# Two blocks of a hybrid network on one core: the order of rounding, scaling and turning the first operand and the state-space output

## The chip, the cores and the metric

The kernel runs on one core of one Trainium2 chip. A time is device microseconds (us) of one execution; three executions give the median. Engines: TensorE (PE, with PEld its weight loads), VectorE (DVE), ScalarE (ACT), GpSimd (POOL) and SyncE (SP), which here issues the loads of the weights.

## The reference

Batch 1, 256 tokens, width 2048, all in float32. Two blocks follow each other. What the change touches lies in the first part of the first block:

```python
a_in = _rmsnorm(h, attn_norm_g)
proj = a_in @ w_in                       # 2048 x (2048 + 3072 + 32 + 3072)
z, xbc, dt_raw, q, k, v = split(proj)
xs, bm, cm = split(silu(causal_dwconv(xbc)))
y = _ssd(xs, dt, a_neg, bm, cm) + d_skip * xs       # 4 groups of 512 channels
y = y * silu(z)
y_ssm = _rmsnorm(y per group of 512, ssm_norm_g)    # one root per token and group
y_att = sliding_window_attention(rmsnorm+rope(q), rmsnorm+rope(k), v)
h = h + concatenate([y_ssm, y_att]) @ w_out
```

After it come a convolved feed-forward layer, a gated embedding, and the second block (gated delta rule, Fourier mixing, MLP). They are not touched.

## The kernel before

**Products.** Every large matrix product is made of float32 values split in two: a rounded part (`hi`, type fp32r) and the rest (`lo`). The weights stream in as 952 slabs of 256 rows by 512 columns (512 KB). A quad is four slabs; `w_raw`, `w_hi` and `w_lo` hold one quad each, so a slab's place is free again when the slab four before it is done. SP loads a slab into `w_raw` once `w_lo` of the slab four before is written. ACT copies `w_raw` to `w_hi` with rounding (`split` on ACT, line 754), DVE subtracts to get `w_lo` (`split` on DVE, line 1341). PE does 12 matmuls of 128x512 per slab (`slab`, lines 2137 and 2142): `hi*hi` and `lo*hi` with `w_hi`, four each, then four with `w_lo`. A chunk is eight slabs: 512 output columns over 2048 rows. The signals `hi_ready`, `lo_ready` and `slab_done` count the slabs, so the order of the calls on ACT and DVE decides in which order slabs and operand tiles come.

**The operand.** The left side of a chunk is `a_hi`, `a_lo`: 16 k-tiles of 128 rows by 256 tokens. `operand_tiles(n, src, ready, i)` on PE turns k-tiles 2i and 2i+1 with four 128x128 transposes (line 2165) into a bank of the accumulator memory; ACT rounds that bank into `a_hi` (`gained`, with the norm's gain, or `rounded_operand`), DVE writes the rest into `a_lo` (`gained_rest` or `rest_of_operand`). The pair of tiles i is the left side of slab i of a chunk. From pair 4 on, PE waits until `a_lo` of pair i-4 is done, since they share a bank. New tiles overwrite the old operand in place.

**The first chunk** (`first_chunk`): PE turns pairs 0 and 1, then for slab s it turns pair s+1 (s from 1 to 6), waits for `a_lo` of pair s, and does slab s. ACT's order is in lines 844 to 851, DVE's in 1459 to 1466. Behind it ACT squares h for the norm, DVE takes the mean, and the narrow product for `dt` (`narrow`) follows.

**The state-space part** runs beside the six chunks of q, k and v (`Q_QKV`), one group g beside chunk g+1. PE calls within a chunk: `decay_rows`, `state` before slab 1, `within(0)` before slab 3, `of_state`, `within(1)` before slab 6. POOL makes `xd`, `xds`, waits for `y_squared`, makes `dx`, multiplies the weights `seg_w` that `within` waits for, and normalizes and rotates q and k (`qk_root`, `qk_scaled`, `qk_rotated`). DVE makes `gated_output(t)` and ACT its square (`square(t)`, sum in `ssm_ss`). When all four groups are squared, POOL takes one root for all (line 637), DVE scales z by root and gain (line 1611), and PE turns z beside the last chunk of v, slabs 3 to 7 (`tiles_of_y`, line 2339). The last pair is turned at the start of the next product, `w_out` (`beside`).

Of the kernel before, what the change touches and what calls it, by code (L numbers as in the profile page):

```python
# [25 lines left out]
ALU = mybir.AluOpType  # L26
# [166 lines left out]
def program(nc, wstream, small, const, out):  # L193

    ctx = ExitStack()
    with ctx:
# [339 lines left out]
        def _(pool):  # L536
# [66 lines left out]
            for g in range(GROUPS):  # L603
# [22 lines left out]
                for t in range(TT):  # L626
# [3 lines left out]
                    if t == 0:  # L630
# [6 lines left out]
            inverse_root(ssm_rs[:].rearrange("p t g -> p (t g)"), ssm_ss[:].rearrange("p t g -> p (t g)"),  # L637
                         TT * GROUPS, 1.0 / NC, EPS, ssm_rstd)
# [108 lines left out]
        def _(act):  # L747
# [217 lines left out]
            split(q + 1, 0, 3)  # L965
            rounded_operand(TR_YSSM, 0, 2)
            split(q + 1, 3, 4)
            rounded_operand(TR_YSSM, 2, 3)
            split(q + 2, 0, 1)
            rounded_operand(TR_YSSM, 3, 5)  # L970
            split(q + 2, 1, 2)
            rounded_operand(TR_YSSM, 5, 6)
            split(q + 2, 2, 3)
            rounded_operand(TR_YSSM, 6, 7)
# [358 lines left out]
        def _(dve):  # L1333
# [125 lines left out]
            gained_rest(TR_ATTN, C_ATTN, 0)  # L1459
            for i in range(QUAD):  # L1460
                gained_rest(TR_ATTN, C_ATTN, i + 1)
                split(0, i, i + 1)
            for i in range(QUAD - 1):
                gained_rest(TR_ATTN, C_ATTN, QUAD + i + 1)
                split(Q_XBC + 1, i, i + 1)
            split(Q_XBC + 1, QUAD - 1, QUAD)
# [100 lines left out]

            def qk_sums(c, t):
# [5 lines left out]
            for g in range(GROUPS):  # L1574
# [24 lines left out]
                gated_output(1)  # L1599
                split(q + 2, 2, 4)  # L1600
# [5 lines left out]
            dve.wait_ge(ssm_rstd, 1)  # L1606
            dve.wait_ge(gain_loaded, 16 * (G_SSM + 1))
            for g in range(GROUPS):
                cols = slice(g * NC, (g + 1) * NC)
                for t in range(TT):  # L1610
                    V.scalar_tensor_tensor(z[:, t, cols], z[:, t, cols], ssm_rs[:, t, g:g + 1], gain[:, cols],
# [1257 lines left out]
```

## Time and profile before

| | before |
|---|---|
| median of 3 runs | 3007.11 us (3005.98 to 3009.41) |
| the profiled execution | 3011.07 us |
| its span | 3009.0 us |
| mean granted TensorE clock | 0.994 |
| PE busy | 2955.5 us (98%) |
| DVE, ACT, POOL busy | 2010.2, 1411.7, 322.5 us |

The profiled execution's own time is its span and some 2 us around it. PE is busy nearly all the time; in the 40 slices of the page only the first is below nine tenths (six), and POOL is busy at eight tenths or more in slices 5 to 7, some 300 to 520 us, where the state-space part runs. PE's busy time does not tell at which clock a matmul ran: the row of the granted clock has 8 tenths in the first slice and 9 in nearly all others.

### The profile page before, as it was taken

The page shows a single profiled execution, that of the slowest core. Times are in us where ns is not written, and L with a number is a line of the kernel's source. Part 1 is how long each engine was busy: PE and PEld are TensorE (multiplying, and loading weights), DVE is VectorE, ACT ScalarE, POOL GpSimd, SP SyncE. Part 2 cuts the span into 40 slices and gives each one's busy share as a digit, 9 for nine tenths or more (in the row PEclk, how much of TensorE's full clock was granted, in tenths as well). Part 3 has the DMA queues.
Part 4 walks back from the last instruction along what each step waited for, and adds up shares of the span by engine and source line. Part 5 has one row for each costly group of instructions (what it writes and reads, how often), then busy time and mean ns, then how long its engine had stood idle before and what let it go on. Part 6 is the DMA issues. An engine that isn't in the chain of part 4 may idle for free.

```text
span 3009.0 us, 43769 instructions
## 1 busy us (share of the span) xinstructions
PE 2955.5 (98%) x15191; PEld 2422.7 (81%) x15191; DVE 2010.2 (67%) x2615; ACT 1411.7 (47%) x1807; POOL 322.5 (11%) x276
## 2 busy tenths in 40 slices
PE   6999999999999999999999999999999999999998
PEld 5888877788888888887878877777888888888886
DVE  3765777756666777776668677777655666666665
ACT  4444445644444444445554554333545444444444
POOL 0001880000000000000000054443000000000000
PEclk8999999999999999999999999999999999999999
DMA  4555444456555555564565533333765565555554
GB/s 167 181 183 188 136 135 150 134 187 217 189 188 188 184 188 181 187 196 146 183 230 179 168 126 126 113 124 112 240 220 193 185 196 188 187 190 188 188 189 140
DMA packets 145142, 525.73 MB, mean 175 GB/s; under 512 B 16416, under 2 KB 17184, under 8 KB 144160
## 3 DMA queue, kind: packets, MB, share of 16 engines
q1 hardware_dynamic: 139760, 503.72, 51.6%
q0 software_dynamic: 1536, 11.78, 1.1%
q10 hardware_dynamic: 3760, 9.05, 0.9%
q8 instruction: 58, 0.95, 0.1%
q14 instruction: 28, 0.23, 0.0%
HBM read 516.09 MB, written 8.39 MB: 174 GB/s over the span
## 4 chain that ended last, share of the span: by engine, by line
PE 91%; DVE 3%; issue 2%; ACT 2%; POOL 1%; DMA 1%; DVEq 0%; ACTq 0%; POOLq 0%; SPq 0%
PE bank L2137 55%; PE bank L2142 27%; PE bank L2234 1%; DVE w_lo L1341 1%; ACT w_hi L754 1%; PE bank L2554 1%; PE bank L2165 1%; DMA w_raw<-weights 1%; PE bank L2583 0%; PE bank L2372 0%; PE bank L2305 0%; PE bank L2466 0%; PE bank L2316 0%; PE bank L2242 0%; DVE delta L1875 0%
## 5 line engine op out<-in xcount | busy, mean ns | idle before, releaser
L1341 DVE TENSOR_TENSOR w_lo<-w_raw,w_hi 128x1024 fp32r<-128x1024 f32 x952 | 1197.3, 1267 | 789.5 <-ACT w_hi L754 788.3
L754 ACT CAST w_hi<-w_raw 128x1024 fp32r<-128x1024 f32 x952 | 1000.1, 1052 | 1408.7 <-PE bank L2142 1394.9
L2137 PE MATMUL bank<-w_hi,a_hi 128*128 128x512 f32 x2816 | 1125.5, 400 | 16.5 <-ACT w_hi L754 14.6
L2137 PE MATMUL bank<-w_hi,a_lo 128*128 128x512 f32 x2816 | 1104.2, 392 | 0.0
L2142 PE MATMUL bank<-w_lo,a_hi 128*128 128x512 f32 x2816 | 761.4, 391 | 0.0
L2137 PEld LDWEIGHTS bank<-w_hi,a_hi 128*128 128x128 f32 x2816 | 531.8, 189 | 136.0 <-DVE a_lo L1355 13.0
L2142 PEld LDWEIGHTS bank<-w_lo,a_hi 128*128 128x128 f32 x2816 | 531.7, 189 | 112.8
L2137 PEld LDWEIGHTS bank<-w_hi,a_lo 128*128 128x128 f32 x2816 | 532.6, 189 | 107.1 <-issue 1.9
L2137 PE MATMUL bank<-w_hi,m_hi 128*128 128x512 f32 x496 | 193.5, 390 | 2.3 <-issue 2.3
L2137 PE MATMUL bank<-w_hi,m_lo 128*128 128x512 f32 x496 | 193.4, 390 | 0.0
L1413 DVE TENSOR_TENSOR h<-h,bank 128x512 f32<-128x512 f32 x236 | 151.1, 682 | 19.6 <-PE bank L2142 19.5
L2137 PE MATMUL bank<-w_hi,f_hi 128*128 128x512 f32 x352 | 138.8, 394 | 0.0
L553 POOL TENSOR_TENSOR rstd<-rstd,neg_half 128x2 f32<-128x2 f32 x6 | 4.8, 798 | 1240.9 <-DVE rstd L1370 1240.9
L2137 PE MATMUL bank<-w_hi,f_lo 128*128 128x512 f32 x352 | 137.1, 390 | 0.0
L2142 PE MATMUL bank<-w_lo,m_hi 128*128 128x512 f32 x496 | 133.5, 391 | 0.0
L2137 PEld LDWEIGHTS bank<-w_hi,m_hi 128*128 128x128 f32 x496 | 93.4, 188 | 21.9 <-issue 2.5
L2142 PEld LDWEIGHTS bank<-w_lo,m_hi 128*128 128x128 f32 x496 | 93.7, 189 | 19.6
L2137 PEld LDWEIGHTS bank<-w_hi,m_lo 128*128 128x128 f32 x496 | 93.4, 188 | 19.4
L2142 PE MATMUL bank<-w_lo,f_hi 128*128 128x512 f32 x352 | 94.2, 389 | 0.0
L2142 PEld LDWEIGHTS bank<-w_lo,f_hi 128*128 128x128 f32 x352 | 66.1, 188 | 13.9
L2137 PEld LDWEIGHTS bank<-w_hi,f_lo 128*128 128x128 f32 x352 | 66.1, 188 | 13.5 <-issue 0.2
L745 POOL TENSOR_TENSOR rstd<-rstd,neg_half 128x1 f32<-128x1 f32 x2 | 1.5, 746 | 704.6 <-DVE rstd L2099 704.6
(397 smaller groups left out, 2489.7 us busy)
## 6 DMA issues: line engine op xcount, KB each, us to landing
w_raw<-weights SPq DMA_DIRECT2D x952, 512.0 KB, 4.1
gate<-gate_st ACTq DMA_DIRECT2D x8, 512.0 KB, 3.9
h<-gate ACTq DMA_DIRECT2D x8, 512.0 KB, 4.7
gain<-gains POOLq DMA_DIRECT2D x3, 1024.0 KB, 6.9
h<-x_tok SPq DMA_DIRECT2D x4, 512.0 KB, 11.1
w_proj_sb<-w_proj POOLq DMA_DIRECT2D x1, 2048.0 KB, 9.8
h_rest<-h POOLq DMA_DIRECT2D x1, 2048.0 KB, 13.2
h<-h_rest POOLq DMA_DIRECT2D x1, 2048.0 KB, 9.6
```

The costliest lines, as they stand in the source:

```text
L553: nc.gpsimd.tensor_tensor(rstd[:, n], rstd[:, n], neg_half[:, 0:TT], ALU.pow).then_inc(rstd_ready, 1)
L745: nc.gpsimd.tensor_tensor(rstd[:, N_OUT, t:t + 1], rstd[:, N_OUT, t:t + 1], neg_half[:, 0:1], ALU.pow).then_inc(rstd_ready, 1)
L754: nc.scalar.copy(w_hi[:, s, :], w_raw[:, s, :]).then_inc(hi_ready, 1)
L1341: V.tensor_tensor(w_lo[:, s, :], w_raw[:, s, :], w_hi[:, s, :].bitcast(F32), ALU.subtract).then_inc(lo_ready, 1)
L1413: V.tensor_tensor(h[:, t, col], h[:, t, col], pair[p][t][:], ALU.add).then_inc(pair_free[p], 1)
L2137: T.matmul(psum[t][:], left[:, t * P:(t + 1) * P], wh, start=start and j == 0 and n == 0, stop=False)
L2142: last = T.matmul(psum[t][:], products[j][0][:, t * P:(t + 1) * P], wl, start=False, stop=stop and j == SLAB_KT - 1)
L2165: last = T.transpose(bank[4 + i % 4][:, k * SEQ + t * P:k * SEQ + (t + 1) * P], src[:, t, (2 * i + k) * P:(2 * i + k + 1) * P], ident[:])
L2234: last = T.transpose(bank[first + ct // 2][:, (ct % 2) * SEQ + t * P:(ct % 2) * SEQ + (t + 1) * P], src[:, t, col0 + ct * P:col0 + (ct + 1 ...
L2554: last = T.matmul(out[r, r], left[:, r], right[:, r], start=True, stop=True)
```

## The change

Three edits, and the orders of the engines that belong together.

1. First chunk: ACT and DVE work on pair i of the k-tiles, then on slab i, for i from 0 to 7 (before: pair i+1, then slab i). PE is not changed there.
2. POOL takes the root of group g-1 during group g, behind `xds` (128x2 each time), and the last one alone; DVE scales z of group g-1 (two instructions) in group g, behind `gated_output(1)`.
3. PE turns one pair of z ahead of each slab 1 to 7 of the last chunk of v (before: pairs 0 and 1 at slab 3, 2 at 4, 3 and 4 at 5, 5 at 6, 6 at 7); ACT and DVE round a pair behind each slab's weight.

```diff
@@ POOL
                 if g:
                     pool.wait_ge(y_squared, TT * g)
+                    inverse_root(ssm_rs[:, :, g - 1], ssm_ss[:, :, g - 1], TT, 1.0 / NC, EPS, ssm_rstd)
@@
             pool.wait_ge(y_squared, TT * GROUPS)
-            inverse_root(ssm_rs[:].rearrange("p t g -> p (t g)"), ssm_ss[:].rearrange("p t g -> p (t g)"),
-                         TT * GROUPS, 1.0 / NC, EPS, ssm_rstd)
+            inverse_root(ssm_rs[:, :, GROUPS - 1], ssm_ss[:, :, GROUPS - 1], TT, 1.0 / NC, EPS, ssm_rstd)
@@ ACT
             gained(TR_ATTN, C_ATTN, 0)
+            split(0, 0, 1, first=True)
+            for s in range(1, QUAD):
+                gained(TR_ATTN, C_ATTN, s)
+                split(0, s, s + 1, first=True)
             for s in range(QUAD):
-                gained(TR_ATTN, C_ATTN, s + 1)
-                split(0, s, s + 1, first=True)
-            for s in range(QUAD - 1):
-                gained(TR_ATTN, C_ATTN, QUAD + s + 1)
+                gained(TR_ATTN, C_ATTN, QUAD + s)
                 split(Q_XBC + 1, s, s + 1)
-            split(Q_XBC + 1, QUAD - 1, QUAD)
@@ DVE, beside chunk g+1
                 gated_output(1)
+                if g:
+                    ssm_normalize(g - 1)
                 split(q + 2, 2, 4)
@@ DVE, last chunk
-            dve.wait_ge(ssm_rstd, 1)
-            ...
-            rest_of_operand(TR_YSSM, 0, 2)
-            ...
+            ssm_normalize(GROUPS - 1)
+            for i in range(KT // 2 - 1):
+                rest_of_operand(TR_YSSM, i, i + 1)
+                split(q + 1 + (i + 1) // QUAD, (i + 1) % QUAD, (i + 1) % QUAD + 1)
@@ PE
-                  between={3: lambda: tiles_of_y(0, 1), 4: lambda: tiles_of_y(2), 5: lambda: tiles_of_y(3, 4),
-                           6: lambda: tiles_of_y(5), 7: lambda: tiles_of_y(6)})
+                  between={i + 1: lambda i=i: tiles_of_y(i) for i in range(KT // 2 - 1)})
```

ACT in the first chunk before: L779 is a pair of k-tiles (two instructions), L754 the rounding of a slab of the weights.

```order
L779 ACTIVATE a_hi<-bank,gain_col_sb 128x256 [waits tr_ready,gain_ready]
L779 ACTIVATE a_hi<-bank,gain_col_sb 128x256
L779 ACTIVATE a_hi<-bank,gain_col_sb 128x256 [waits tr_ready]
L779 ACTIVATE a_hi<-bank,gain_col_sb 128x256
L754 CAST w_hi<-w_raw 128x1024 [waits raw_loaded0]
L779 ACTIVATE a_hi<-bank,gain_col_sb 128x256 [waits tr_ready]
L779 ACTIVATE a_hi<-bank,gain_col_sb 128x256
L754 CAST w_hi<-w_raw 128x1024 [waits raw_loaded1]
```

The same place now:

```order
L779 ACTIVATE a_hi<-bank,gain_col_sb 128x256 [waits tr_ready,gain_ready]
L779 ACTIVATE a_hi<-bank,gain_col_sb 128x256
L754 CAST w_hi<-w_raw 128x1024 [waits raw_loaded0]
L779 ACTIVATE a_hi<-bank,gain_col_sb 128x256 [waits tr_ready]
L779 ACTIVATE a_hi<-bank,gain_col_sb 128x256
L754 CAST w_hi<-w_raw 128x1024 [waits raw_loaded1]
L779 ACTIVATE a_hi<-bank,gain_col_sb 128x256 [waits tr_ready]
L779 ACTIVATE a_hi<-bank,gain_col_sb 128x256
```

Each slab's rounding has moved up by one pair of k-tiles.

DVE in the last chunk of v before, from the second slab's weight on: L1341 writes `w_lo` of a slab, L1611 scales z, L1347 writes `a_lo` of a pair.

```order
L1341 TENSOR_TENSOR w_lo<-w_raw,w_hi 128x1024 [waits hi_ready]
L1611 SCALAR_TENSOR_TENSOR z<-z,ssm_rs,gain 128x512 x2
L1341 TENSOR_TENSOR w_lo<-w_raw,w_hi 128x1024 [waits hi_ready]
L1611 SCALAR_TENSOR_TENSOR z<-z,ssm_rs,gain 128x512 x2
L1341 TENSOR_TENSOR w_lo<-w_raw,w_hi 128x1024 [waits hi_ready]
L1611 SCALAR_TENSOR_TENSOR z<-z,ssm_rs,gain 128x512 x2
L1347 TENSOR_TENSOR a_lo<-bank,a_hi 128x512 [waits a_hi_ready] x3
```

Now (L1565 scales z, L1340 writes `a_lo`, L1334 `w_lo`):

```order
L1565 SCALAR_TENSOR_TENSOR z<-z,ssm_rs,gain 128x512 [waits ssm_rstd]
L1565 SCALAR_TENSOR_TENSOR z<-z,ssm_rs,gain 128x512
L1340 TENSOR_TENSOR a_lo<-bank,a_hi 128x512 [waits a_hi_ready]
L1334 TENSOR_TENSOR w_lo<-w_raw,w_hi 128x1024 [waits hi_ready]
L1340 TENSOR_TENSOR a_lo<-bank,a_hi 128x512 [waits a_hi_ready]
L1334 TENSOR_TENSOR w_lo<-w_raw,w_hi 128x1024 [waits hi_ready]
L1340 TENSOR_TENSOR a_lo<-bank,a_hi 128x512 [waits a_hi_ready]
```

Six of the eight scalings have moved into the groups before, and the pairs alternate with the slabs.

POOL beside chunks 2 to 4 now; L547 and L548 are the new root, between `xds` (L618) and `dx` (L624):

```order
L614 TENSOR_TENSOR work<-xs,dt 128x512
L618 TENSOR_TENSOR work<-work,ds 128x512 [waits xd_ready]
L547 TENSOR_SCALAR ssm_rs<-ssm_ss 128x2 [waits y_squared]
L548 TENSOR_TENSOR ssm_rs<-ssm_rs,neg_half 128x2 [waits pool_step]
L624 TENSOR_TENSOR stage<-xs,row_sb 128x512 x2
L630 TENSOR_TENSOR work<-work,cv_act 128x1024 [waits seg_exp]
```

Two instructions stand ahead of `dx` and of `seg_w` (L630) that did not before; the wait for `y_squared` stood there already.

## Rows read from the trace of the kernel before

**Rows 1.** The page: busy time, share of the span and instructions.
```profile
PE 2955.5 (98%) x15191; PEld 2422.7 (81%) x15191; DVE 2010.2 (67%) x2615; ACT 1411.7 (47%) x1807; POOL 322.5 (11%) x276
```

**Rows 2.** Waits, 0 to 60 us: us in total, times, longest.
```profile
PE bank L2137 <- ACT w_hi L754: 14.6, 7, 2.9
```

**Rows 3.** Timeline of PE, first chunk: start, duration, line, count, idle before.
```profile
16.55 0.60 PE L2165 MATMUL bank<-ident_sb,h 128*128 128x128 f32 x4
19.11 0.47 PE L2137 MATMUL bank<-w_hi,a_hi 128*128 128x512 f32 x1 [1.95 <-ACT w_hi L754]
...
23.52 0.60 PE L2165 MATMUL bank<-ident_sb,h 128*128 128x128 f32 x4
```

**Rows 4.** Windows, first chunk: length, busy by engine, granted clock, DMA.
```profile
19.80:23.20 3.40, 3.40 (x10) 2.62 (x9) 0.42 (x1) 0.00 (x0) 0.00 (x0) 0.52 0.76 259
23.20:26.60 3.40, 1.45 (x9) 1.05 (x8) 1.51 (x3) 1.77 (x3) 0.00 (x0) 0.99 0.00 1
```

**Rows 5.** Timeline of ACT, end of the first chunk.
```profile
52.77 1.99 ACT L754 CAST w_hi<-w_raw 128x1024 fp32r<-128x1024 f32 x2
54.66 0.63 ACT L763 ACTIVATE xs<-h 128x512 f32<-128x512 f32 x1
```

**Rows 6.** Timeline of PE, end of the first chunk and start of the narrow product.
```profile
53.96 0.47 PE L2137 MATMUL bank<-w_hi,a_hi 128*128 128x512 f32 x1 [1.95 <-ACT w_hi L754]
...
56.77 0.39 PE L2137 MATMUL bank<-w_hi,a_hi 128*128 128x512 f32 x1
...
60.96 0.31 PE L2213 MATMUL bank<-a_hi,w_hi 128*32 128x256 f32 x1 [1.31 <-DVE w_lo L1469]
```

**Rows 7.** DMA issues, 14.3 to 15 us: slab 4's load, median us to landing.
```profile
w_raw<-weights SPq DMA_DIRECT2D x1, 512.0 KB, 7.5
```

**Rows 8.** Timeline of PE, last chunk of v.
```profile
422.33 0.39 PE L2137 MATMUL bank<-w_hi,a_hi 128*128 128x512 f32 x1
...
431.57 1.09 PE L2165 MATMUL bank<-ident_sb,z 128*128 128x128 f32 x8 [0.92 <-DVE z L1611]
...
441.66 0.63 PE L2165 MATMUL bank<-ident_sb,z 128*128 128x128 f32 x4 [2.60 <-DVE a_lo L1347]
...
449.66 0.60 PE L2165 MATMUL bank<-ident_sb,z 128*128 128x128 f32 x4
...
452.85 0.60 PE L2165 MATMUL bank<-ident_sb,z 128*128 128x128 f32 x4
```

**Rows 9.** Windows, last chunk of v.
```profile
442.80:446.40 3.60, 3.60 (x10) 2.77 (x9) 2.52 (x3) 0.11 (x1) 3.44 (x6) 0.53 0.32 100
446.40:456.00 9.60, 9.60 (x49) 7.79 (x47) 5.53 (x7) 5.18 (x7) 5.11 (x12) 1.00 0.55 186
```

**Rows 10.** Timeline of POOL and DVE, end of group 3 and last chunk.
```profile
425.45 1.65 POOL L548 TENSOR_TENSOR ssm_rs<-ssm_rs,neg_half 128x8 f32<-128x8 f32 x1
...
440.33 0.76 POOL L598 TENSOR_TENSOR xs<-qkv,cos 128x64 f32<-128x64 f32 x1
441.05 0.31 POOL L598 TENSOR_TENSOR xs<-qkv,sin 128x64 f32<-128x64 f32 x1
...
430.11 1.41 DVE L1611 SCALAR_TENSOR_TENSOR z<-z,ssm_rs,gain 128x512 f32<-128x512 f32 x2
```

**Rows 11.** Line 553, the root of 128x2: duration in ns, min/median/max.
```profile
L553 POOL TENSOR_TENSOR rstd<-rstd,neg_half x6: 695/716/1245, 60.2 to 2296.2; 128x2 f32<-128x2 f32 x6
```

**Rows 12.** Timeline of PE and POOL, group 2.
```profile
364.85 1.12 PE L2324 MATMUL bank<-work,b_tok 128*128 128x512 f32 x2 [0.95 <-POOL work L618]
...
371.30 1.89 PE L2316 MATMUL bank<-work 128*128 128x64 f32 x16
...
367.74 3.39 POOL L629 TENSOR_TENSOR work<-work,cv_act 128x1024 f32<-128x1024 f32 x1
```

**Rows 13.** Waits and windows, groups 0 to 3.
```profile
POOL qk_rs L576 <- DVE qk_ss L1572: 8.7, 3, 4.0
...
360.00:366.00 6.00, 5.05 (x26) 3.71 (x25) 2.85 (x3) 4.67 (x9) 5.84 (x8) 1.00 0.56 175
```

More of the change, by code:

```diff
@@ L963, in _ @@
                 qk_squares(GROUPS, t)
[L965 to L974, printed above, removed]
+            for i in range(KT // 2 - 1):
+                split(q + 1 + i // QUAD, i % QUAD, i % QUAD + 1)
+                rounded_operand(TR_YSSM, i, i + 1)
             split(q + 2, 3, 4)
@@ L1458, in _ @@
             dve.wait_ge(gain_ready, 1)
-            gained_rest(TR_ATTN, C_ATTN, 0)
             for i in range(QUAD):
-                gained_rest(TR_ATTN, C_ATTN, i + 1)
+                gained_rest(TR_ATTN, C_ATTN, i)
                 split(0, i, i + 1)
-            for i in range(QUAD - 1):
-                gained_rest(TR_ATTN, C_ATTN, QUAD + i + 1)
+            for i in range(QUAD):
+                gained_rest(TR_ATTN, C_ATTN, QUAD + i)
                 split(Q_XBC + 1, i, i + 1)
-            split(Q_XBC + 1, QUAD - 1, QUAD)
             mean_square(N_ATTN)
@@ L1566, in _, with ssm_normalize @@
             qkv_evac(0)
+            def ssm_normalize(g):
+                cols = slice(g * NC, (g + 1) * NC)
+                dve.wait_ge(ssm_rstd, g + 1)
+                if g == 0:
+                    dve.wait_ge(gain_loaded, 16 * (G_SSM + 1))
+                for t in range(TT):
+                    V.scalar_tensor_tensor(z[:, t, cols], z[:, t, cols], ssm_rs[:, t, g:g + 1], gain[:, cols],
+                                           ALU.mult, ALU.mult).then_inc(normed, 1)
             def qk_sums(c, t):
@@ L1605, in _ @@
                 qk_sums(GROUPS, t)
-            dve.wait_ge(ssm_rstd, 1)
[L1607 to L1611, printed above, removed]
-                                           ALU.mult, ALU.mult).then_inc(normed, 1)
-                if g < GROUPS - 1:
-                    split(q + 1, g + 1, g + 2)
-            rest_of_operand(TR_YSSM, 0, 2)
-            rest_of_operand(TR_YSSM, 2, 3)
-            split(q + 2, 0, 1)
-            rest_of_operand(TR_YSSM, 3, 5)
-            split(q + 2, 1, 2)
-            rest_of_operand(TR_YSSM, 5, 6)
-            split(q + 2, 2, 3)
-            rest_of_operand(TR_YSSM, 6, 7)
-            split(q + 2, 3, 4)
+            ssm_normalize(GROUPS - 1)
+            for i in range(KT // 2 - 1):
+                rest_of_operand(TR_YSSM, i, i + 1)
+                split(q + 1 + (i + 1) // QUAD, (i + 1) % QUAD, (i + 1) % QUAD + 1)
             qkv_evac(5)
-            rest_of_operand(TR_YSSM, 7, 8)
+            rest_of_operand(TR_YSSM, KT // 2 - 1)
             scale = float(HD ** -0.5)
```

## The prediction, made before the changed kernel ran

> **What bounds the kernel now.** I read the page first: TensorE is busy for 98% of the span [rows 1], so nothing off its path is worth anything, and the share hides at which clock it ran. Next the waits of the first 60 us: seven waits of TensorE for a rounded slab, 14.6 us together [rows 2], the first 2.9 us, the other six 1.95 us each. The timeline shows why. At 16.55 us TensorE turns the next pair of k-tiles and then needs slab 1, whose rounding stands on ScalarE behind that very pair; slab 1 starts at 19.11 us, and the next turning is at 23.52 us [rows 3]. So a slab takes 23.52 - 16.55 = 6.97 us. A second cost lies on top: the granted clock alternates between half and full (0.52, then 0.99, [rows 4]). The half is 1.2 GHz; it follows each stretch with a wait and lifts in each dense one. The same two things are seen once more in the last chunk of v: a wait of 0.92 us for scaled z, one of 2.60 us for `a_lo`, and behind it 3.6 us at 0.53 of the clock [rows 8, 9]. Everywhere else in this chunk the clock is 1.00, and the stretch where one pair is turned per slab runs without a wait at 452.85 - 449.66 = 3.19 us per slab with its turning [rows 8, 9]. That is the rate that both edited places can reach.
>
> **The first chunk (edit 1).** No instruction is added or taken away on any engine; slab s is rounded before pair s+1 instead of behind it. Slab 0 waits for its load and starts as before. Up to the turning at 16.55 us nothing changes, and the four w_lo matmuls before it are dense. There are six turnings, of pairs 2 to 7, hence five intervals between them. Before: 6.97 us each; now I take 3.19 us. Over one interval before, from 19.8 to 26.6 us, ScalarE works 1.77 us and VectorE 0.42 + 1.51 = 1.93 us [rows 4], so both fit into 3.19. The last turning moves from 51.4 to 32.5 us: 5 x (6.97 - 3.19) = 18.9 us. TensorE's eighth slab, at 56.77 us before [rows 6], would start at 32.5 + 0.35 + 2.81 = 35.7 (2.81 is 56.77 - 53.96), 21.1 us earlier. It does not get all of that, for the narrow product waits for a chain on ScalarE and VectorE (squares, mean, rest of the small weight). That chain starts at 54.66 us behind two roundings, 1.99 us [rows 5]; now one of them is already done, so it starts 18.9 + 1.0 = 19.9 us earlier. The narrow product at 60.96 us moves to 41.1, and TensorE's idle before it grows from 1.3 to some 2.6 us. What was covered by TensorE's slowness is thus the ScalarE chain, and it becomes late next. All behind it is shifted by 19.9 us.
>
> The cover for the loads: slab 4 is issued at 14.45 us and lands 7.5 us later [rows 7], at 22; it is wanted at about 24 (pair 4 is turned at 16.55 + 2 x 3.19 = 22.9 and rounded first). Later loads are issued one per slab, and 512 KB per 3.19 us is 164 GB/s, under what the row of 259 GB/s shows as possible [rows 4]. If slab 4 came late, the cost would be what it lacks, within 2 us.
>
> The clock: behind the 2.60 us wait in the last chunk 3.6 us ran at 0.53, a loss of 3.6 x (1 - 0.53) = 1.7 us [rows 8, 9]. The new idle of 2.6 us before the narrow product is as long. Bounds 0 and 1.7 us; I take 1.0 us. Term: -19.9 + 1.0 = -18.9 us.
>
> The Trainium skill (TensorE: Matmul & The Clock Gate, Part 1) says that half speed is the default state and that sustained activity lifts it. By it the dense chunk would stay at full clock, as the rows of 446 to 456 us do; no row shows it for the first chunk itself.
>
> **The last chunk of v (edit 3, with the scalings of edit 2).** Before it runs from 422.33 to the turning of pair 7 at 452.85 us, 30.5 us [rows 8]. Now: a first slab of 2.81 us, then seven of 3.19 us, 25.1 us. In this gain of 5.4 us lie the 0.92 and the 2.60 us waits and the 1.7 us lost at half clock. What could be late instead: pair 4 waits for `a_lo` of pair 0 on VectorE, which stands behind the scaling of group 3. That scaling starts where the first one started, at 430.1 us [rows 10], and takes 1.41; `a_lo` of pair 0 is out by about 432.5, and pair 4 is turned ahead of slab 5, at about 437.9. Pairs 6 and 7, the only ones that need group 3, come at 444 us or later. Pair 7 and what follows it are not changed. Bounds: 3.5 us (only the two waits) and 6 us; I take 5.4.
>
> **The groups (edit 2).** POOL does 128x2 roots three times more: 0.72 us for the power [rows 11] and for the multiply-add ahead of it about what POOL's smallest product takes, 0.31 us [rows 10]: 1.0 us each; the last root is 128x2 instead of 128x8 (1.65 us, [rows 10]), 0.9 less, at a point where nobody waits for it. Behind each new root on POOL's queue stand `dx`, `seg_w` and all of q's and k's work, and TensorE waits for `seg_w` in `within`. In groups 1 and 3 POOL goes idle for `qk_ss` right behind `seg_w` (the 8.7 us of three waits less the longest, 4.0, in group 0, are 4.7 us for these two, [rows 13]): it is ahead of the engines that it serves, and I take the root as absorbed. In group 2 it is not: `seg_w` ends at 367.74 + 3.39 = 371.13 and `within(0)` starts at 371.30 us [rows 12]; the full 1.0 us comes onto TensorE. Two more places are as tight: `state` of group 2 already waits 0.95 us for `xds` [rows 12], and `state` of group 3 stands behind the same work of POOL one group on. What reaches them is how much the moved scalings slow POOL. VectorE takes 1.41 us per group for two scalings [rows 10]; it is busy for 2.85 of 6 us there and has the time [rows 13]. POOL's small products took 0.76 us beside VectorE's scaling and 0.31 us right behind it [rows 10], so 0.45 us per instruction that meets it; I take one such meeting in each of the two places, 0.45 each. Term: +1.0 + 0.9 = +1.9 us. Bounds: 0 (all absorbed) and 3 x (1.0 + 1.41) = 7.2 us, each root and both scalings in full on TensorE in every group.
>
> The rows say that a POOL product met by a scaling grows by 0.45 us. The Trainium skill (SBUF — State Buffer, the section on the two separate sides) has a harsher rule: GpSimd and a VectorE instruction with two SBUF inputs exclude each other for a whole instruction. By it POOL could lose 1.4 us in each of the two tight places, and the term would be 3.8 instead of 1.9 us; the trace agrees in kind, not in that size.
>
> **Sum.** -18.9 - 5.4 + 1.9 = -22.4 us. On the profiled execution: 3011.07 - 22.4 = 2988.7 us. That execution lies 4.0 us above the median of the runs, so for the median I subtract the same: 3007.11 - 22.4 = 2984.7 us.
>
> **Rivals.**
> 1. The clock does not follow. For it speaks that in the first 50 us it came back only for a stretch at a time. If it keeps alternating, only the waits go: 6 x 1.95 = 11.7 us in place of 18.9. Sum -11.7 - 5.4 + 1.9 = -15.2, 2991.9 us. Against it: it rose in every dense stretch.
> 2. POOL is later than I take it, at the upper bound of 7.2 us: -18.9 - 5.4 + 7.2 = -17.1, 2990.0 us. For it: POOL is busy 5.84 of 6 us around 360 us [rows 13], and its durations vary. Against: it needs the cost in all three groups, two of which have idle time.
> 3. Slower than before: the same waits for POOL, spread over groups 1 to 3, throw the clock back as in the first chunk. Half clock costs 12 matmuls twice their time, some 2.4 us per slab. The gains are 24.3 us, so it decides from ten of the 24 slabs at half clock; with all 24, 58 us are lost and the kernel takes some 3041 us. Against it: a wait of 0.95 us at 364 us left the clock at 1.00 [rows 13], and the wait must be near 2 us in almost every slab, which POOL's seven microseconds can't give.
> 4. The change does nothing at the start, because something else holds slabs 1 to 7 (loads): only -5.4 + 1.9 = -3.5, 3003.6 us. The loads landed before they are needed, so little speaks for it.
>
> **Chances.** Forecast 0.75 (its own range 2980.5 to 2988.5), rival 1 0.12, rival 2 0.09, rival 3 0.01, rival 4 0.03. The bounds of the unknown costs (clock 0 to 1.7, chunk 3.5 to 6, POOL 0 to 7.2) give -25.9 to -14.5 at the extremes; with rival 1 the upper end is the same. Range: 2980.5 to 2992.5 us. Less than 0.2%, 6 us, is about what a measurement of this kernel can't tell from no change. Faster by more than that: 0.75 + 0.12 + 0.09 = 0.96; within it, rival 4: 0.03; slower 0.01.
>
> **What would show it.** In the profile of the changed kernel: TensorE's waits for ScalarE's L754 in the first 60 us are one, of some 2.9 us, and six are gone; turnings follow at 3.2 us; the window from 20 to 38 us has a granted clock of 1.00; the narrow product starts at about 41 us behind an idle of 2.6 us. The last chunk of v takes 25 us from its first slab to the turning of pair 7, with no window below 1.00. In group 2, `state` waits some 1.4 us and `within(0)` about 1 us for POOL. Wrong would be: turnings at 5 us or more (clock or loads), a narrow product after 43 us, waits for POOL of more than 3 us together, or a new wait for `a_lo` or z in the last chunk.

## The result and the profile after

| | before | after |
|---|---|---|
| median | 3006.99 us (3005.98 to 3009.41) | 2989.9 us (2987.65 to 2990.37) |
| the profiled execution | 3011.07 us | 2989.82 us |
| its span | 3009.0 us | 2987.9 us |
| mean granted clock | 0.994 | 0.998 |

The ratio is 0.9939, with a 95% interval of 0.9924 to 0.9955: the kernel became faster by 17 us by the medians and 18 us by the ratio, and the interval reaches from 13.5 to 23 us. In a later job the changed kernel was run again: 0.9936 (0.9922 to 0.9949), 19.5 us by the medians. The two profiled executions lie 21.25 us apart. The forecast of 2984.7 us had the direction, and its range of 2980.5 to 2992.5 us holds the time; the median is 5.2 us above the forecast. In the first of the three later jobs one of 21 executions of the kernel before took 12256.76 us, and the ratios there leave it out.

The page after. It answers to [rows 1], and below it stands its row of the granted clock:

```profile
PE 2944.5 (99%) x15191; PEld 2415.3 (81%) x15191; DVE 2008.6 (67%) x2615; ACT 1411.4 (47%) x1807; POOL 328.9 (11%) x282
...
PEclk9999999999999999999999999999999999999999
```

TensorE has as many matmuls as before and 11 us less busy time, so some of them ran faster. The rest of the 21 us was idle time. POOL has six instructions and 6.4 us more.

Waits of TensorE from 0 to 60 us (total, times, longest), which answer to [rows 2]:

```profile
PE bank L2125 <- ACT w_hi L754: 3.0, 1, 3.0
```

Timeline of TensorE there (start, duration, line, count, idle before), for [rows 3, 6]:

```profile
15.98 0.60 PE L2153 MATMUL bank<-ident_sb,h 128*128 128x128 f32 x4
19.18 0.60 PE L2153 MATMUL bank<-ident_sb,h 128*128 128x128 f32 x4
...
31.99 0.60 PE L2153 MATMUL bank<-ident_sb,h 128*128 128x128 f32 x4
...
40.59 0.30 PE L2201 MATMUL bank<-a_hi,w_hi 128*32 128x256 f32 x1 [2.51 <-DVE w_lo L1460]
```

Six of the seven waits are gone, the turnings follow at 3.20 us in place of 6.97, and the narrow product starts at 40.59 us, 20.4 us earlier. Of these 20.4 us, 0.6 lie ahead of the first turning (15.98 in place of 16.55 us), which the edit does not reach. The idle time ahead of the narrow product has grown from 1.31 to 2.51 us.

Windows of the same kernel (length, busy by engine, granted clock, DMA share, GB/s), for [rows 4]:

```profile
20.00:25.00 5.00, 5.00 (x26) 4.09 (x25) 3.15 (x6) 3.37 (x6) 0.00 (x0) 1.00 0.83 319
...
35.00:40.00 5.00, 3.08 (x14) 2.23 (x12) 1.15 (x4) 5.00 (x17) 0.12 (x1) 1.00 0.41 136
```

The clock is 1.00 in both. From 35 to 40 us ScalarE is busy for all 5.00 us and TensorE for 3.08: that is the chain of squares that is now late.

The last chunk of v, timeline of TensorE, for [rows 8]:

```profile
407.37 0.60 PE L2153 MATMUL bank<-ident_sb,z 128*128 128x128 f32 x4
...
429.68 0.60 PE L2153 MATMUL bank<-ident_sb,z 128*128 128x128 f32 x4
...
433.93 0.63 PE L2344 MATMUL bank<-ident_sb,qkv 128*128 128x128 f32 x4 [0.90 <-POOL xs L648]
```

Eight turnings 3.19 us apart and none with a wait; the chunk starts at 404.65 us, 25.0 us before its last turning, against 30.5 before.

Timeline of TensorE in groups 1 to 3, its waits for GpSimd, for [rows 12]:

```profile
319.29 2.00 PE L2304 MATMUL bank<-work 128*128 128x64 f32 x16 [0.36 <-POOL work L630]
...
345.00 1.13 PE L2312 MATMUL bank<-work,b_tok 128*128 128x512 f32 x2 [0.93 <-POOL work L618]
...
351.92 2.00 PE L2304 MATMUL bank<-work 128*128 128x64 f32 x16 [0.31 <-POOL work L630]
...
377.65 1.12 PE L2312 MATMUL bank<-work,b_tok 128*128 128x512 f32 x2 [0.93 <-POOL work L618]
...
384.57 2.00 PE L2304 MATMUL bank<-work 128*128 128x64 f32 x16 [0.31 <-POOL work L630]
```

Five waits, 2.84 us together, against one of 0.95. They are 1.9 us longer, but the groups cost more than that. The last chunk of v starts 17.7 us earlier (404.65 in place of 422.33 us, [rows 8]), so 20.4 - 17.7 = 2.7 us of the lead were lost in the groups: a wait costs TensorE more time than the idle time that is counted for it. At about 434 us the changed kernel is 20.4 - 2.7 + 5.5 - 0.3 = 22.9 us ahead (0.3 for a longer way from the last turning to L2344). At the end it is 21.1 us ahead. In the rest of the program, which the change doesn't touch, the execution of the changed kernel has a window at 0.97 of the clock (1460 to 1560 us; 1.00 before), and its wait for `s_act` is 3.2 us instead of 2.6.

### The profile page after: what moved, and what is told of

It is laid out like the page before. It is cut to its first block, busy times and chain, and to the rows that moved or that the text cites. A ratio compares the mean times of both kernels' runs of the same rounds, so it can differ in the third digit from the quotient of the medians.

```text
span 2987.9 us, 43775 instructions
## 1 busy us (share of the span) xinstructions
PE 2944.5 (99%) x15191; PEld 2415.3 (81%) x15191; DVE 2008.6 (67%) x2615; ACT 1411.4 (47%) x1807; POOL 328.9 (11%) x282
## 4 chain that ended last, share of the span: by engine, by line
PE 88%; POOL 4%; DVE 3%; issue 2%; ACT 1%; DMA 1%; DVEq 0%; ACTq 0%; POOLq 0%; SPq 0%
PE bank L2125 54%; PE bank L2130 27%; PE bank L2222 1%; DVE w_lo L1334 1%; PE bank L2541 1%; ACT w_hi L754 1%; DMA w_raw<-weights 1%; PE bank L2153 1%; POOL work L630 1%; POOL xs L598 1%; POOL qkv L587 0%; PE bank L2570 0%; POOL qk_rs L577 0%; PE bank L2359 0%; PE bank L2453 0%
## 5 line engine op out<-in xcount | busy, mean ns | idle before, releaser
L1334 DVE TENSOR_TENSOR w_lo<-w_raw,w_hi 128x1024 fp32r<-128x1024 f32 x952 | 1198.7, 1269 | 789.0 <-ACT w_hi L754 787.4
L754 ACT CAST w_hi<-w_raw 128x1024 fp32r<-128x1024 f32 x952 | 1000.2, 1052 | 1407.7 <-PE bank L2130 1394.6
L1406 DVE TENSOR_TENSOR h<-h,bank 128x512 f32<-128x512 f32 x236 | 151.1, 681 | 19.6 <-PE bank L2130 19.5
L2125 PEld LDWEIGHTS bank<-w_hi,f_lo 128*128 128x128 f32 x352 | 66.1, 188 | 13.5 <-issue 0.2
## 6 DMA issues: line engine op xcount, KB each, us to landing
h<-x_tok SPq DMA_DIRECT2D x4, 512.0 KB, 10.9
```

The lines of the kernel that those rows point to most:

```text
L754: nc.scalar.copy(w_hi[:, s, :], w_raw[:, s, :]).then_inc(hi_ready, 1)
L1334: V.tensor_tensor(w_lo[:, s, :], w_raw[:, s, :], w_hi[:, s, :].bitcast(F32), ALU.subtract).then_inc(lo_ready, 1)
L1406: V.tensor_tensor(h[:, t, col], h[:, t, col], pair[p][t][:], ALU.add).then_inc(pair_free[p], 1)
L2125: T.matmul(psum[t][:], left[:, t * P:(t + 1) * P], wh, start=start and j == 0 and n == 0, stop=False)
```

## The experiments

Each was timed against the kernel before on the same chip. The kernel before came out at 3008.95, 3009.7 and 3009.03 us in the three jobs.

### One edit at a time

**Edit 1 alone.** ACT and DVE round pair i of the first chunk ahead of slab i, the rest is the kernel before.

```diff
-            gained(TR_ATTN, C_ATTN, 0)
-            for s in range(QUAD):
-                gained(TR_ATTN, C_ATTN, s + 1)
-                split(0, s, s + 1, first=True)
+            gained(TR_ATTN, C_ATTN, 0)
+            split(0, 0, 1, first=True)
+            for s in range(1, QUAD):
+                gained(TR_ATTN, C_ATTN, s)
+                split(0, s, s + 1, first=True)
...
```

> The kernel before with edit 1 alone (first chunk, a pair of k-tiles and its own slab in turn). Theory: the first chunk carries the larger gain, and does it alone: narrow product at about 40.6 us instead of 61.0, TensorE's six waits of 1.95 us gone, the clock full from the second slab on. About 18.5 us less than before in the medians (17 to 21), and the last chunk of v still takes 30.5 us with its waits of 0.9 and 2.6 us. Rival (the loss at half clock moves elsewhere and is not recovered): only the waits, 11.7 us less.

Measured: 2992.53 us (2991.34 to 2995.03), ratio 0.9945 (0.9932 to 0.9959), 16.4 us, a little under the 17 to 21 expected. It is clearly more than the 11.7 us of the rival. Its turnings follow at 3.2 us (3.4 the first time), and the last chunk still has its waits of 0.91 and 2.60 us. Timeline of TensorE:

```profile
41.56 0.42 PE L2211 MATMUL bank<-a_hi,w_hi 128*32 128x256 f32 x1 [2.51 <-DVE w_lo L1467]
```

The narrow product's first matmuls took 0.42 us here and 0.30 in the changed kernel, behind the same idle time of 2.51 us. The window shows it (columns as above):

```profile
40.00:50.00 10.00, 7.96 (x52) 6.63 (x53) 8.56 (x22) 8.03 (x13) 1.25 (x1) 0.83 0.38 124
```

In the changed kernel the same window has 1.00. So half clock can follow the 2.51 us, at a cost of 10 x 0.17 = 1.7 us. It did in this execution and in that of edits 1 and 3 below (0.83 in the same window), but not in the two profiled ones of the changed kernel.

**Edit 2 alone.** Roots per group and z scaled in the next group's time; the turnings stay as they were.

```diff
                 if g:
                     pool.wait_ge(y_squared, TT * g)
+                    inverse_root(ssm_rs[:, :, g - 1], ssm_ss[:, :, g - 1], TT, 1.0 / NC, EPS, ssm_rstd)
@@ DVE
                 gated_output(1)
+                if g:
+                    ssm_normalize(g - 1)
                 split(q + 2, 2, 4)
...
-            for g in range(GROUPS):
-                ...scale z of group g...
-                if g < GROUPS - 1:
-                    split(q + 1, g + 1, g + 2)
+            ssm_normalize(GROUPS - 1)
+            split(q + 1, 1, 4)
```

> The kernel before with edit 2 alone: a root per group on GpSimd, z of group g-1 scaled in group g, but TensorE turns z at slabs 3 to 7 as before. Theory A (the waits in the last chunk came from the six scalings that stood ahead of a_lo on VectorE): the 0.9 us wait goes and the 2.6 us wait shrinks below 1 us, the clock stays full, the chunk takes some 25.5 us; the groups cost 2.7 us more; sum -2.3 us. Theory B (the waits came from turning two pairs at a time): the 2.6 us wait stays, the chunk takes 29 to 30 us, and the kernel is 1 to 2 us slower than before.

Measured: 3005.99 us (3003.32 to 3009.68), ratio 0.9993 (0.9984 to 1.0002): some 2 us, which its interval does not tell from nothing. Timeline of TensorE in its last chunk:

```profile
430.85 1.03 PE L2169 MATMUL bank<-ident_sb,z 128*128 128x128 f32 x8
...
447.66 0.60 PE L2169 MATMUL bank<-ident_sb,z 128*128 128x128 f32 x4
451.63 0.63 PE L2361 MATMUL bank<-ident_sb,qkv 128*128 128x128 f32 x4 [0.63 <-DVE a_lo L1347]
```

That is theory A. The old order, with two pairs at slabs 3 and 5, runs without a wait as well, and the chunk takes some 25 us, as in the changed kernel. So the gain of the last chunk comes from the scalings having left it, not from the one-pair order.

**Edits 1 and 3, without 2.** One root for all groups, all scalings at the last chunk's start, and then one pair per slab.

```diff
-                    inverse_root(ssm_rs[:, :, g - 1], ssm_ss[:, :, g - 1], TT, 1.0 / NC, EPS, ssm_rstd)
...
-                if g:
-                    ssm_normalize(g - 1)
...
-            ssm_normalize(GROUPS - 1)
+            for g in range(GROUPS):
+                ssm_normalize(g)
             for i in range(KT // 2 - 1):
                 rest_of_operand(TR_YSSM, i, i + 1)
                 split(q + 1 + (i + 1) // QUAD, (i + 1) % QUAD, (i + 1) % QUAD + 1)
```

> The changed kernel without edit 2: the first chunk and the turning of one pair per slab as changed, but one root for all groups and all eight scalings in the last chunk. Theory: edit 3 can't stand without edit 2, since pair 0 is now wanted ahead of slab 1, at about 405 us, and z of group 0 is scaled some 7 us later: one wait of 6 to 8 us for z, half clock behind it (1.7 us), and the last chunk takes 32 us or more; the groups lose the 2.7 us of cost. Sum against before: -20.4 -2 (clock and groups, at most) +2 or so: 17 to 20 us less than before, 2 to 5 us more than the changed kernel in the last chunk. Rival (no coupling, one pair per slab is what counts): chunk of 25 us, and 2.7 us faster than the changed kernel.

Measured: 2996.12 us (2994.06 to 2998.35), ratio 0.9956 (0.9942 to 0.9969), so 3.6 us slower than edit 1 alone. Its 12.8 us under the kernel before are fewer than the 17 to 20 expected. TensorE, last chunk:

```profile
413.59 1.11 PE L2152 MATMUL bank<-ident_sb,z 128*128 128x128 f32 x4 [6.34 <-DVE z L1565]
...
437.48 0.60 PE L2152 MATMUL bank<-ident_sb,z 128*128 128x128 f32 x4
```

The first turning asks for z 6.34 us too early; the last stands at 437.48, against 434.61 us with edit 1 alone. Edit 3 needs edit 2: without it, one wait of 6.34 us stands in the place of the two of 0.91 and 2.60. No run shows a gain of edit 3 of its own.

### The wait and the clock told apart

**The kernel before with its waits filled.** The order is left as it was. Behind each turning of pairs 2 to 7 of the first chunk TensorE does eight more matmuls of 128x512 into a free bank; their result is not used.

```diff
                         operand_tiles(n, src, ready, s + 1)
+                        if n == TR_ATTN:
+                            for _ in range(FILL):          # FILL = 8
+                                T.matmul(bank[2][:], a_hi[:, 0, 0:P], a_hi[:, 0:2, :]..., start=True, stop=True)
```

> The kernel before, with eight matmuls of 512 columns into an unused bank behind each of the turnings of pairs 2 to 7 of the first chunk (1.7 us at full clock); their results are not used. No wait is removed: ScalarE's order is that of before. Theory (waits and half clock are two costs, of 11.7 and 7.2 us): with TensorE busy in the gap the clock stays full, a slab's period falls from 6.97 to about 5.4 us, and the narrow product comes at 52 to 54 us; some 8 us less than before. Rival (the clock does not come back whatever TensorE does there, or the gain came from the waits alone): the period stays at 7 us or grows, no gain or slower.

Measured: 3000.69 us (2999.98 to 3005.24), ratio 0.9975 (0.9966 to 0.9984): adding work made the kernel 7.5 us faster by the ratio. TensorE, first chunk, and its window:

```profile
15.61 0.60 PE L2166 MATMUL bank<-ident_sb,h 128*128 128x128 f32 x4
15.96 2.09 PE L2188 MATMUL bank<-a_hi 128*128 128x512 f32 x8
18.16 0.47 PE L2138 MATMUL bank<-w_hi,a_hi 128*128 128x512 f32 x1
...
20.99 0.60 PE L2166 MATMUL bank<-ident_sb,h 128*128 128x128 f32 x4
...
52.13 0.31 PE L2217 MATMUL bank<-a_hi,w_hi 128*32 128x256 f32 x1 [1.31 <-DVE w_lo L1470]
```

```profile
16.00:52.00 36.00, 34.17 (x154) 26.14 (x152) 14.68 (x23) 17.68 (x37) 0.58 (x1) 1.00 0.45 151
```

The slab starts 2.55 us behind the turning, as before (16.55 to 19.11 us, [rows 3]): the filling fits in the wait, and the rounding sets the time. From there to the next turning it takes 2.83 us in place of 4.41. So an interval is 5.38 us, at full clock and with the rounding just as late as before. Of an interval of 6.97 us, 6.97 - 5.38 = 1.59 is the half clock and 5.38 - 3.20 = 2.18 the wait: over five intervals 7.9 and 10.9 us. The forecast had 18.9 us for them, of which rival 1 kept 7.2 for the clock and 11.7 for six waits. The narrow product moved by 8.8 us here, 60.96 - 52.13, of which 0.9 lay ahead of the first turning (15.61 in place of 16.55 us).

### The profile taken again

The kernel before and the changed one, unchanged, in another job.

> The kernel before once more, for a second profile. The forecast was made against one execution, 4 us above the median. Theory (where the clock rises and falls against the waits of the first chunk differs between executions, and the profiled one had it at its worst): the narrow product starts 1 to 3 us earlier than 60.96 us here, as it does in the profile of edit 2 alone, whose first chunk is the same. Rival (the 4 us lie elsewhere): 61.0 us again, and the difference is found later in the program.

> The changed kernel once more, in five rounds against the kernel before. Theory: ratio 0.9935 to 0.9945, some 17 to 19 us; the narrow product at 40.6 or 41.6 us behind an idle of 2.5 us, and in some executions at half clock for a part (the profile of edit 1 alone had it, this one had not). Rival (the difference of the profiles is the true one): 21 us or more, ratio 0.993.

Measured: the kernel before ran once, at 3010.4 us; the changed one at 2990.2 us (2988.83 to 2991.55), ratio 0.9936 (0.9922 to 0.9949). The waits repeat to 0.1 us: 14.5 us in seven for the rounded slab, 2.6, 1.0 and 0.9 before; 2.9, 2.5, 1.9 and 0.9 after. What does not repeat is where the clock rises and falls. The kernel before had its last wait of the first chunk here:

```profile
54.81 0.47 PE L2137 MATMUL bank<-w_hi,a_hi 128*128 128x512 f32 x1 [1.96 <-ACT w_hi L754]
```

That is 0.85 us later than in [rows 6], and the narrow product starts at 61.94 us, 1.0 us later; I had expected it 1 to 3 us earlier. In edit 2 alone, whose first chunk is that of before, the turnings went from 15.73 to 49.00 us, 2.4 us earlier than in the first profile: 0.8 at the first of them, and one interval of 5.40 us instead of 6.97. The kernel with the roots per group (below), whose first chunk is also that of before, has its last turning at 49.12 us. The same code thus came to its last turning of the first chunk up to 3.3 us apart (49.00 and 52.26 us), with the same waits.

### What is late next

**Squares of h earlier.** ScalarE squares one piece of h (two instructions) behind each slab of the first chunk's second half, instead of all behind the last.

```diff
             for s in range(QUAD):
                 gained(TR_ATTN, C_ATTN, QUAD + s)
                 split(Q_XBC + 1, s, s + 1)
-            for c in range(DC):
-                act.wait_ge(piece_loaded[c], 16)
-                squares(h, xs, c)
+                act.wait_ge(piece_loaded[s], 16)
+                squares(h, xs, s)
```

> The changed kernel with ScalarE's squares of h moved into the first chunk, one piece behind each of the slabs 4 to 7 (ScalarE has 1.4 us idle per slab there, two squares take 1.2). Theory (the idle of 2.5 us ahead of the narrow product is ScalarE's chain, now late next): it shrinks to 0.5 us or less, the narrow product starts at some 38.5 us, and the clock stays full behind it; 2 to 3 us less than the changed kernel. Rival (the chain is held by VectorE or the loads of the small weights): no gain.

Measured: 2985.6 us (2983.26 to 2988.9), ratio 0.9924 (0.9911 to 0.9938). It ran again beside the kernel with one root:

> The changed kernel with the squares of h moved into the first chunk, as the comparison for the kernel with one root, on the same chip. Both theories: 3 to 5 us less than the changed kernel, 2984 to 2987 us.

2984.5 us (2983.05 to 2986.49), ratio 0.9918 (0.9904 to 0.9931). The first of ScalarE's squares in the run of 2985.6 us, and what follows the narrow product on TensorE:

```profile
24.67 0.64 ACT L763 ACTIVATE xs<-h 128x512 f32<-128x512 f32 x1
```

```profile
44.12 0.30 PE L2206 MATMUL bank<-ident_sb,sp 32*128 32x32 f32 x2 [0.45 <-ACT sp L867]
```

The squares start 9.6 us earlier than in the changed kernel (34.30 us), in time where ScalarE had room; the wait of 2.51 us ahead of the narrow product is gone, and the transposes of `sp` come at 44.12 instead of 46.83 us. In the first job this version is 4.6 us under the changed kernel (2990.2), in the second 24.5 us under the kernel before (3009.03). It beats both. I had expected 2 to 3 us. Up to `sp` the profiles show 2.7 us of the 4.6, and 2.9 us at about 434 us (431.05 in place of 433.93); where the rest lies is not shown.

**state, within(0) and of_state one slab later.**

```diff
-                      between={0: lambda: decay_rows(0), 1: state, 3: second_tile, 4: of_state, 6: lambda: within(1)})
+                      between={0: lambda: decay_rows(0), 2: state, 4: second_tile, 5: of_state, 6: lambda: within(1)})
```

> The changed kernel with TensorE's calls for the state-space groups one slab later (state ahead of slab 2, within(0) and decay_rows(1) ahead of slab 4, of_state ahead of slab 5; within(1) stays). Theory (GpSimd is only late against these places, by up to 2 us at the third group): the five waits of 2.8 us together go, some 2.5 us less than the changed kernel. Rival (GpSimd is the bound of the groups, 32.6 us of work per group against some 31 of TensorE, so a wait moved is a wait found at within(1)): the waits turn up there and nothing is gained.

Measured: 2991.13 us (2987.66 to 2993.87), ratio 0.9936 (0.9922 to 0.995): no gain over the changed kernel. The last of its three waits for GpSimd, with what follows it:

```profile
367.08 2.92 PE L2304 MATMUL bank<-work 128*128 128x64 f32 x16 [1.46 <-POOL work L630]
...
370.76 0.63 PE L2125 MATMUL bank<-w_hi,a_hi 128*128 128x512 f32 x1
371.18 0.63 PE L2125 MATMUL bank<-w_hi,a_lo 128*128 128x512 f32 x1
```

Five waits of 2.84 us became three of 3.49: 1.42 and 1.46 us at `within(1)`, 0.61 at `within(0)`. The last one is followed by matmuls 0.42 us apart in place of 0.23: half clock (0.50 from 370 to 373 us). From group 2 to 3 GpSimd still needs 32.62 us. A consumer that asks later does not help where the producer has no idle time left.

### Root or scaling

**Roots per group, z scaled at the end as before.** The order on DVE is that of the kernel before; only the roots move.

```diff
                     pool.wait_ge(y_squared, TT * g)
+                    inverse_root(ssm_rs[:, :, g - 1], ssm_ss[:, :, g - 1], TT, 1.0 / NC, EPS, ssm_rstd)
...
-            dve.wait_ge(ssm_rstd, 1)
+            dve.wait_ge(ssm_rstd, GROUPS)
```

> The kernel before with one root per group on GpSimd (part of edit 2), but z scaled at the end as before. Theory A (the roots themselves fill GpSimd): TensorE's waits for `xds` and `seg_w` in groups 1 to 3 come to 1.6 to 3 us together, as in the changed kernel (2.84 us), against 0.95 before; the last chunk keeps its wait of 2.6 us; 3007 to 3011 us. Theory B (the scalings beside GpSimd slow it): the waits stay near 1 us, and the power of 128x2 takes 0.7 us in every group instead of 1.73 us.

Measured: 3011.51 us (3010.14 to 3015.16), ratio 1.001 (1.0001 to 1.0019), 2.5 us slower by the medians, just clear of no change. Waits of TensorE from 250 to 420 us:

```profile
PE bank L2316 <- POOL work L630: 2.0, 3, 0.8
```

TensorE's first `state` (group 0) and its last `within(1)` (group 3), in the kernel before, in this one and in the changed one:

```profile
301.96 1.02 PE L2324 MATMUL bank<-work,b_tok 128*128 128x512 f32 x2
...
415.06 1.89 PE L2316 MATMUL bank<-work 128*128 128x64 f32 x16
```

```profile
300.02 1.02 PE L2324 MATMUL bank<-work,b_tok 128*128 128x512 f32 x2
...
415.27 1.89 PE L2316 MATMUL bank<-work 128*128 128x64 f32 x16
```

```profile
281.53 1.02 PE L2312 MATMUL bank<-work,b_tok 128*128 128x512 f32 x2
...
397.38 1.89 PE L2304 MATMUL bank<-work 128*128 128x64 f32 x16
```

POOL's `xds` (L618) in groups 2 and 3, first the kernel before, then this one with its power (L548), then the changed one with its power:

```profile
363.75 1.04 POOL L618 TENSOR_TENSOR work<-work,ds 128x512 f32<-128x512 f32 x1
394.81 1.04 POOL L618 TENSOR_TENSOR work<-work,ds 128x512 f32<-128x512 f32 x1
```

```profile
361.63 1.04 POOL L618 TENSOR_TENSOR work<-work,ds 128x512 f32<-128x512 f32 x1
...
393.97 1.04 POOL L618 TENSOR_TENSOR work<-work,ds 128x512 f32<-128x512 f32 x1
...
395.38 0.71 POOL L548 TENSOR_TENSOR ssm_rs<-ssm_rs,neg_half 128x2 f32<-128x2 f32 x1
```

```profile
343.91 1.04 POOL L618 TENSOR_TENSOR work<-work,ds 128x512 f32<-128x512 f32 x1
...
345.31 1.73 POOL L548 TENSOR_TENSOR ssm_rs<-ssm_rs,neg_half 128x2 f32<-128x2 f32 x1
...
371.47 0.65 POOL L600 TENSOR_TENSOR qkv<-xs 128x64 f32<-128x64 f32 x1
372.08 1.30 POOL L601 TENSOR_TENSOR qkv<-xs 128x64 f32<-128x64 f32 x1
...
376.55 1.04 POOL L618 TENSOR_TENSOR work<-work,ds 128x512 f32<-128x512 f32 x1
```

VectorE of the changed kernel at the same two places, `w_lo`, and the two scalings with the `w_lo` behind them:

```profile
345.25 1.23 DVE L1334 TENSOR_TENSOR w_lo<-w_raw,w_hi 128x1024 fp32r<-128x1024 f32 x1 [2.66 <-ACT w_hi L754]
...
370.41 1.54 DVE L1565 SCALAR_TENSOR_TENSOR z<-z,ssm_rs,gain 128x512 f32<-128x512 f32 x2
371.87 1.34 DVE L1334 TENSOR_TENSOR w_lo<-w_raw,w_hi 128x1024 fp32r<-128x1024 f32 x1
```

`dx` (L623, L624) of group 1, in the kernel before and in the one with the roots alone:

```profile
332.20 2.04 POOL L623 TENSOR_TENSOR stage<-xs,row_sb 128x512 f32<-128x512 f32 x2
```

```profile
331.33 3.04 POOL L624 TENSOR_TENSOR stage<-xs,row_sb 128x512 f32<-128x512 f32 x2
```

From group 2 to 3 GpSimd needs 31.06 us before, 32.34 with the root, 32.64 in the changed kernel. So a root lengthens it by 1.3 us and the moved scalings by another 0.3. On TensorE the waits are 0.95, 1.96 and 2.84 us, 1.0 more by the roots and 0.9 by the scalings. The time from the first `state` to the last `within(1)` tells more than the waits: 113.10, 115.25 and 115.85 us, so the roots cost 2.15 us and the scalings 0.60. It repeats to 0.1 us in four more profiles with the old roots and to 0.2 us in four more with edit 2. Both theories hold a part, and the roots the larger one.

The root costs more than its own 1.0 us because of what it delays. In group 1 of the kernel before, `dx` was over when a `w_lo` of VectorE started (334.19 us). Behind the root `dx` meets that `w_lo` and takes 3.04 us in place of 2.04; in group 3 it is the same (3.03 in place of 2.04).

The power of 128x2 takes 1.73 us beside the `w_lo` of 345.25 us and 0.71 us with the roots alone. No scaling meets it there, but the scalings bring the meeting about: edit 2 alone differs from the roots alone only by them, and its power takes 1.73 us in groups 2 and 3 too. Of the two last rotations the first (0.65 us) meets the second scaling and the other (1.30 us) the `w_lo` behind it; with the roots alone each takes 0.32 us. That is 1.31 us more, but the period grew by only 0.3, since other meetings with VectorE went away: in the same period `seg_w` takes 2.39 us in place of 3.37, and `dx` 2.50 in place of 3.03.

**One root for groups 0 to 2, in group 3.** On top of the earlier squares.

```diff
-                    inverse_root(ssm_rs[:, :, g - 1], ssm_ss[:, :, g - 1], TT, 1.0 / NC, EPS, ssm_rstd)
+                if g == GROUPS - 1:
+                    ...one root of ssm_ss[:, :, 0:g], 128x6...
@@ DVE: z of group 0 behind gated_output(0), of 1 behind gated_output(1) of group 3
+            ssm_normalize(GROUPS - 2)
             ssm_normalize(GROUPS - 1)
```

> The changed kernel with the earlier squares of h, and with one root of 128x2x3 for groups 0 to 2 in group 3 instead of three roots; z of group 0 is scaled behind the first gated output of group 3, of group 1 behind the second, of group 2 and 3 in the last chunk. Theory A (GpSimd's roots cost TensorE about 1 us each in groups 1 to 3): two roots less, waits in these groups under 1.8 us together, last chunk without a wait as now; 1 to 3 us less than the kernel with the squares alone in this job. Theory B (the sum of GpSimd's slowed work counts, wherever the scalings stand, and group 3 takes all of it): no difference over 0.7 us, and a longer wait for `xds` or `seg_w` in group 3.

Measured: 2985.07 us (2984.57 to 2986.55), ratio 0.9922 (0.9908 to 0.9935), against 2984.5 us for the squares alone: no gain in the medians. TensorE's first `state` and last `within(1)`:

```profile
279.82 1.02 PE L2317 MATMUL bank<-work,b_tok 128*128 128x512 f32 x2
...
394.34 1.89 PE L2309 MATMUL bank<-work 128*128 128x64 f32 x16
```

That is 114.52 us, against 115.85 with the squares alone (278.85 and 394.70 us): the groups became 1.3 us shorter. The waits fell from 2.8 to 2.1 us, in group 3 from 1.26 to one of 1.15. So group 3 does not pay what groups 1 and 2 save, as theory B had it, and the last chunk begins only 0.36 us earlier because this execution came to its narrow product 1.0 us later (38.90 in place of 37.93 us). The waits stayed above the 1.8 us of theory A. Two executions can't show the whole kernel's gain, and five runs each spread over 2 to 3.4 us: whether one root is worth its 1.3 us stays open.

## Why the prediction was right

**First chunk: -19.9 us forecast, -20.4 measured.** Each step held. Turnings at 3.20 us (forecast 3.19), the one remaining wait 3.0 us (2.9), no late load, the clock at 1.00, and the narrow product at 40.59 us (41.1; 41.13 in the second profile) behind 2.51 us of idle time (2.6). The half microsecond more lies ahead of the first turning, where I had said that nothing changes. That the covered chain on ScalarE would be late next is shown by taking it away: 4.6 us more. The clock's price, put at 1.0 us (bounds 0 and 1.7), was 0 in the two profiled executions of the changed kernel and 1.7 us in two others with an idle time as long. The filled kernel's window has 1.00 with the roundings as late as before. What the Trainium skill says of it (TensorE: Matmul & The Clock Gate, Part 1, sustained activity lifts the clock) agrees with that. Rival 1, the clock that keeps alternating, is out; it would have left those 7.9 us in the kernel.

**Last chunk: -5.4 forecast, -5.5 measured.** No wait for `a_lo` or z. But the forecast put the gain under edit 3 with the scalings of edit 2, and did not ask which of them earns it: edit 2 does, alone.

**Groups: +1.9 forecast, +2.7 measured.** The waits alone grew by 1.9 us; that this is the forecast's figure is luck, for the waits fell elsewhere than I had said, and the time lost is more than the waits. I had the whole root at `within(0)` of group 2 and nothing in groups 1 and 3, since GpSimd waited there for `qk_ss` [rows 13]. That wait stands behind `seg_w` and says nothing of how early `seg_w` is. Before, `seg_w` ended 1.5 us ahead of `within(0)` in group 1 (337.68 and 339.21 us) and 1.2 us in group 3 (401.18 and 402.36), enough for a root of 1.0 us. But with the roots alone, and `dx` slowed behind them, `seg_w` comes 2.0 us later in these groups, counted from `xds`, and `within(0)` waits 0.35, 0.83 and 0.78 us. In the changed kernel each waits 0.3 us, `state` of group 2 waits 0.93 us as before (I had priced 0.45 more there), and `state` of group 3, which did not wait before, waits 0.93 us, because group 2 has no idle time and hands its lateness on. I had priced that place at 0.45.

A meeting, too, costs more than the 0.45 us that I took: the power grew by 1.02 us beside a `w_lo` of 1.23, a rotation by 0.98 beside one of 1.34. The Trainium skill's rule (SBUF — State Buffer, two separate sides) is nearer to that than I weighed it. The 3.8 us that the prediction worked out from it for the term are still too much, since the moved scalings partly take the place of other meetings. Rival 2, POOL at 7.2 us, did not come.

**The sum.** By 434 us: -22.9 us measured against -19.9 + 1.0 - 5.4 + 1.9 = -22.4. Up to there the working was half a microsecond off, partly because its errors cancel: 1.5 us more in the first chunk with its clock, 0.8 and 0.3 us less behind it. What moved the median, 17.1 and 19.5 us in two jobs, away from it is two things of a size that I had put at nothing. The profiled execution of before stood 4 us above the median and that of after stood on it, and I carried its gain over in full. And clock and waits in the untouched part shift from execution to execution: between the two profiled ones 1.8 us of the lead were lost there. The first median of the kernel before is also of four executions only; in the three later jobs it was 2 to 3 us higher. That these things fill the gap is an account of profiles, not shown by an experiment; the forecast ratio, 0.9925, lies inside both measured intervals.

**What the time alone would have said.** 2989.9 us lies outside the 2980.5 to 2988.5 us that I gave to the forecast itself, and on rival 2's 2990.0 us. The range held it because of the rivals' costs. Only the traces tell that the mechanism was the forecast's: the groups cost 2.7 us and not 7.2. The upper end of the range was also not what I said of it: with rival 1 and the same bounds for the rest, -11.7 - 3.5 + 7.2 = -8.0 us, 2999.1 us, and not the same end.

**Rivals 3 and 4.** Rival 3, slower by half clock in the groups, did not come: waits of 0.93 us left the clock at 1.00. I had said that it needs waits near 2 us; where they were made longer, the clock dropped behind one of 1.46 us. Rival 4, nothing gained at the start, is refuted by edit 1 alone.

## What to carry to other kernels

Where a producer engine prepares two things for a consumer that can go on with either, order them by when the consumer needs each, not by when each becomes possible; a wait of two microseconds that recurs can cost nearly as much again in the clock (here 1.59 us beside 2.18), and useless matmuls put in its place tell the two costs apart. When such a wait goes, look at once for the chain that its slowness covered and start it earlier. Before moving work onto an engine that "has idle time", check the length of its period, group to group, and how early each of its results is, and not its waits: once that period is the longest, moving the consumer later gains nothing, and a small instruction put in the middle can also slow the ones behind it. And measure the time of a stretch beside its waits; here they grew by 1.9 us and the stretch by 2.75.

## What the runs showed of the hardware

- Half clock in the first chunk starts and ends at other places from execution to execution of the same code: intervals of 6.97 and 5.40 us, and a last turning up to 3.3 us apart.
- The same idle time of 2.51 us ahead of the narrow product was followed by matmuls of 0.42 us in the kernel with edit 1 alone (clock 0.83 from 40 to 50 us) and of 0.30 us in the changed kernel (1.00). With state and its followers one slab later, the clock fell behind a wait of 1.46 us and not behind one of 1.42 us; behind the waits of 0.93 us of the changed kernel it did not fall.
- A short GpSimd instruction met by VectorE can take more than twice its time: 0.71 to 1.73 us beside a `w_lo` of 1.23 us, and 0.32 to 1.30 us beside one of 1.34 us. It grows by about 1 us, somewhat less than VectorE's instruction takes. Two instructions of `dx` grew from 2.04 to 3.04 us together.
